# Gate and up passes of a mixture-of-experts layer in four 32-slot column tiles, and a gather that rotates over four PSUM banks

## What is computed

```python
def expert_block(args):
    rows, e = args
    xb = x_pad[rows]
    h = jax.nn.silu(xb @ w_gate[e]) * (xb @ w_up[e])
    return h @ w_down[e]
...
routed = jax.ops.segment_sum(yb * row_g[:, None].astype(yb.dtype), row_t, num_segments=n + 1)[:n]
shared = (jax.nn.silu(xt @ ws_gate) * (xt @ ws_up)) @ ws_down
```

## Time and profile before

| what | value |
|---|---|
| median of 3 runs | 1186.67 us (1184.7 to 1186.79) |
| span of the profiled execution, first to last instruction | 1183.3 us |
| what lies around the span, if that execution took the median | 3.4 us |
| PE matmuls busy | 1149.2 us (97%) |
| weight loads of PE | 688.0 us (58%) |
| VectorE, ScalarE | 347.2 us, 300.0 us |
| DMA | 449.12 MB, mean 380 GB/s |
| MoE of layer 0, gate pass of unit 0 to last down pass | 134 to 572 us |
| MoE of layer 1 | 732 to 1169 us |

### The profile page before, as it was taken

How to read it: one execution, slowest core, us unless ns; L and a number is a source line. 1 busy time by engine, 2 the same in 40 slices (tenths; PEclk the granted TensorE clock), 3 DMA queues, 4 the chain that set the end, 5 groups by cost and what they waited for, 6 DMA issues and landing times.

```text
span 1183.3 us, 22174 instructions
## 1 busy us (share of the span) xinstructions
PE 1149.2 (97%) x8846; PEld 688.0 (58%) x8846; DVE 347.2 (29%) x912; ACT 300.0 (25%) x713; POOL 56.4 (5%) x100
## 2 busy tenths in 40 slices
PE   9999999999999999999999999999999899999995
PEld 6865755555555555554787647555555555555552
DVE  0445522222122212121523557221222222121224
ACT  1454222212122212121214533122221212221222
POOL 1431100000001000000011001000000010000000
PEclk9999999999999999999999999999999999999998
DMA  9945999999999999999990558999999999999995
GB/s 375 418 161 185 349 418 426 428 428 428 429 428 421 429 426 427 426 426 418 406 364 2 230 233 343 408 426 426 429 429 428 428 423 427 426 426 428 428 423 204
DMA packets 42732, 449.12 MB, mean 380 GB/s; under 512 B 4512, under 2 KB 4896, under 8 KB 14240
## 3 DMA queue, kind: packets, MB, share of 16 engines
q1 hardware_dynamic: 41648, 443.30, 89.8%
q10 hardware_dynamic: 1008, 4.73, 1.0%
HBM read 446.96 MB, written 1.05 MB: 379 GB/s over the span
## 4 chain that ended last, share of the span: by engine, by line
PE 85%; DMA 9%; DVE 3%; ACT 1%; issue 1%; DVEq 0%; SPq 0%; ACTq 0%
PE bank L1301 18%; PE bank L1328 17%; PE bank L1364 17%; PE bank L848 7%; PE bank L867 6%; PE bank L1372 5%; PE bank L906 4%; DMA store<-in_w_gate 4%; DMA store<-in_w_down 3%; DMA store<-in_w_in_b 2%; PE bank L1337 2%; PE bank L1196 1%; PE bank L1066 1%; PE bank L1077 1%; ACT work L1498 1%
## 5 line engine op out<-in xcount | busy, mean ns | idle before, releaser
L1301 PE MATMUL bank<-store,work 128*64 128x256 f32 x1984 | 227.8, 382 | 5.3 <-DMA store<-in_w_gate 5.3
L1328 PE MATMUL bank<-store,work 128*64 128x256 f32 x1952 | 225.3, 379 | 6.2 <-issue 6.2
L1364 PE MATMUL bank<-store,work 128*32 128x512 f32 x1888 | 218.4, 595 | 3.1 <-ACT work L1498 2.9
L1301 PEld LDWEIGHTS bank<-store,work 128*64 128x64 f32 x1984 | 137.0, 137 | 116.1 <-issue 41.1
L1328 PEld LDWEIGHTS bank<-store,work 128*64 128x64 f32 x1952 | 145.0, 137 | 75.7 <-issue 11.6
L2030 DVE SCALAR_TENSOR_TENSOR yhalf<-bank,gcol,yhalf 128x512 fp32r<-128x512 f32 x124 | 92.9, 751 | 219.1 <-ACT yhalf L1664 219.1
L2022 DVE TENSOR_TENSOR work<-work,bank 128x256 f32<-128x256 f32 x64 | 27.0, 422 | 346.9 <-PE bank L1328 346.9
L1664 ACT ACTIVATE yhalf<-bank,gcol 128x512 fp32r<-128x512 f32 x124 | 85.1, 688 | 172.1 <-PE bank L1364 172.1
L1364 PEld LDWEIGHTS bank<-store,work 128*32 128x32 f32 x1888 | 56.1, 109 | 122.4 <-issue 110.7
L1498 ACT ACTIVATE work<-bank 128x512 f32<-128x512 f32 (+4 forms) x177 | 78.0, 441 | 105.8 <-PE bank L848 47.3
L1498 ACT ACTIVATE back<-bank 128x128 fp32r<-128x128 bf16 x64 | 17.8, 278 | 282.0 <-PE bank L1269 282.0
(11 more groups left out here) (185 smaller groups left out, 822.7 us busy)
## 6 DMA issues: line engine op xcount, KB each, us to landing
store<-in_w_down SPq DMA_DIRECT2D x56, 2048.0 KB, 17.7
store<-in_w_gate SPq DMA_DIRECT2D x56, 2048.0 KB, 17.7
store<-in_w_up SPq DMA_DIRECT2D x52, 2048.0 KB, 19.2
store<-in_w_up SPq DMA_DIRECT2D x18, 1024.0 KB, 10.5
store<-in_w_gate SPq DMA_DIRECT2D x12, 1024.0 KB, 8.5
store<-in_w_in_b SPq DMA_DIRECT2D x3, 3072.0 KB, 22.4
store<-in_w_out SPq DMA_DIRECT2D x4, 2048.0 KB, 14.2
store<-in_w_down SPq DMA_DIRECT2D x6, 1024.0 KB, 11.7
```

The costliest lines, as they stand in the source:

```text
L1301: last = pe.matmul(gate_bank[slots_of(e), 0:HID], xg[:, k, slots_of(2 * j + e)], w[e][:, k, :], start=(k == 0), stop=(k == KT - 1))
L1328: last = pe.matmul(up_bank[slots_of(e), 0:HID], xg[:, k, slots_of(2 * j + e)], w[e][:, k, :], start=(k == 0), stop=(k == KT - 1))
L1364: last = pe.matmul(yb[half][rows_of(t, e), :], hT[b][:, f, slots_of(e, t)], w[e][:, f, half * 512:half * 512 + 512], start=(f == 0), stop= ...
```

## The change

Gate and up no longer use one 64-column tile for each expert, but two 32-column tiles for each, one for each token tile. The 64 partitions of an expert and their order stay the same, and each 32-slot tile streams the same 256 weight columns. So a pass has 32 products in the code where it had 16.

The gather's chunks take the banks 0, 3, 1, 2, 0, 3, 1, 2 in place of 0, 1, 2, 0, 1, 2, 0, 1. Four waits follow the banks: the wait for `back_ready` and `gcol_ready` (bank 1) moves from chunk 1 to chunk 2, that for `hT_ready` (bank 2) from chunk 2 to chunk 3; the gate pass of an octet's first unit now also waits before its first matmul until chunk 5 (bank 3, which is the gate bank) is copied out; and the two halves of the down pass wait for chunks 4 and 6, both copied out by ScalarE, in place of chunk 6 and VectorE's chunk 7.

```diff
-        gather_bank = (0, 1, 2, 0, 1, 2, 0, 1)
+        gather_bank = (0, 3, 1, 2, 0, 3, 1, 2)
...
                         if k == 2 and backs is not None:
-                            pe.wait_ge(s_("hT_ready"), backs)
-                        if k == 1 and backs is not None:
                             pe.wait_ge(s_("back_ready"), backs + 1)
                             pe.wait_ge(s_("gcol_ready"), backs + 1)
+                        if k == 3 and backs is not None:
+                            pe.wait_ge(s_("hT_ready"), backs)
...
-                def slots_of(e, t=None):
-
-
-                    first, n = (e * SLOTS, SLOTS) if t is None else (e * SLOTS + t * TILE_SLOTS, TILE_SLOTS)
-                    return slice(first, first + n)
+                def slots_of(e, t):
+
+                    first = e * SLOTS + t * TILE_SLOTS
+                    return slice(first, first + TILE_SLOTS)
...
-                        if j == 0 and k == 0 and first:
-                            chunk_out(O, 3)
+                        if j == 0 and k == 0:
+                            chunk_out(O, 3 if first else 5)
...
                         for e in range(2):
-                            last = pe.matmul(gate_bank[slots_of(e), 0:HID], xg[:, k, slots_of(2 * j + e)], w[e][:, k, :],
-                                             start=(k == 0), stop=(k == KT - 1))
+                            for t in range(TT):
+                                last = pe.matmul(gate_bank[slots_of(e, t), 0:HID], xg[:, k, slots_of(2 * j + e, t)], w[e][:, k, :],
+                                                 start=(k == 0), stop=(k == KT - 1))
...
                         for e in range(2):
-                            last = pe.matmul(up_bank[slots_of(e), 0:HID], xg[:, k, slots_of(2 * j + e)], w[e][:, k, :],
-                                             start=(k == 0), stop=(k == KT - 1))
+                            for t in range(TT):
+                                last = pe.matmul(up_bank[slots_of(e, t), 0:HID], xg[:, k, slots_of(2 * j + e, t)], w[e][:, k, :],
+                                                 start=(k == 0), stop=(k == KT - 1))
...
                     for half in range(2):
-                        if half == 0:
-                            pe.wait_ge(s_("xg_act"), 4 * gathers + 1)
-                        else:
-                            pe.wait_ge(s_("xg_dve"), 4 * gathers + 1)
+                        pe.wait_ge(s_("xg_act"), 4 * gathers + half)
+                        if half == 1:
                             pe.wait_ge(s_("back_ready"), turned + 1)
                             pe.wait_ge(s_("gcol_ready"), turned + 1)
```

## The result

The changed kernel takes 1190.5 us (median of 5 runs, 1189.9 to 1191.8), the kernel before beside it 1186.0 us (5 runs): a ratio of 1.0044, 95% interval 1.0032 to 1.0055. It is slower by 5.2 us by that ratio; the forecast was 1188.8 us. The profiled execution has a span of 1190.0 us and took 1191.84 us, so 1.84 us lie around a span, where the forecast had put 3.4.

The account below looks back on a forecast made before the run. The prediction took the full DMA as the bound: +2.4 us for code, -0.17 and -0.1 made +2.1 on a 1183.3 us span, 1185.4, plus 3.4 around it: 1188.8 us. Its 8-in-10 range was 1185.6 to 1192.4 us.

Parts of the forecast that it names:

- The bound: Both MoE layers: the DMA is full at about 427 GB/s; a unit takes 14.7 us to load, 12.23 us on PE.
- the waits marked "issue": PE waits before an up pass, counted as waits for weights within 11.5 us over both layers.
- The rival that PE sets the end: Whole kernel: PE's savings count in full, 14.4 us less, giving 1172.3 us; chance 0.08.
- Part 1: Gate and up passes: 64 matmuls of 128x32 replace 32 of 128x64 at the same stream time, 0 us.
- The rival of 61 ns for one: Gate and up passes: PE can't keep pace for 128 matmuls, 0.45 us more a pass, 1207 us; chance 0.06.
- Parts 2 and 3: Down-to-gate saves 0.17 us at each place, only the last counting (-0.17 us); gather's up to 0.3 us is hidden, 0.
- Part 4: PE's code: 6144 more instructions, about 24 packets of 16 KB; 22 under full DMA cost +2.4 us (0.9 to 3.3).
- my upper bound of 0.15: Code fetch under full DMA: the most one packet costs, in us, around an estimate of 0.11.
- dips in the middle of the MoE: Sign that the forecast is wrong: the DMA rate dips there or falls below 420 GB/s, a lost lead.
- about 13 us of other loads are always queued ahead: DMA queue: a 2 MB load lands 17.7 us after issue but takes 4.9 us, so the DMA has no gaps.
- The wrong 3.4 us: Time around the profiled span, added to 1185.4 us to give 1188.8 us.
- the refetched loop: PE loop over octets 1 to 3: each further pass brings 6 packets again, +2.6 us, 1191.5 us; chance 0.17.

## Why the prediction was right, and what it mis-sized

**The bound: right.** PE has slack against the DMA while the kept pair is 16. PE's gains turned into waits in the changed kernel (28.1 us for 11.5) and with the banks alone (17.8). That the waits marked "issue" are waits for weights, as the forecast assumed, the trace of the changed kernel bears out: the five between 237 and 350 us end at 264.42, 279.11, 308.47, 323.15 and 337.84 us, each 0.09 us after the last part of a 2 MB load has landed, and no code comes in that stretch for which PE could have waited. The rival that PE sets the end fell; it isn't a property of the passes, though, but of this place of the kept pair, as the runs with pair 20 show.

**Part 1, the shape at 0: right.** 64 narrow matmuls are repeated every 3.45 us over two passes. The rival of 61 ns for one would have given 3.9 us, and the estimate that I drew from the Trainium skill, "TensorE: Matmul & The Clock Gate" (Wait — 56ns, not 53.3ns?), 4.0 us. Measured is 3.45 us/64 = 54 ns. So the rival's 61 ns fell, and the 62 ns, which the Trainium skill states there for hardware decode switched off, don't set the pace here; no run shows which setting holds. The forecast's own row gives 16 x 0.22 = 3.5 us for a pass, not quite the 3.45 that it wrote down; the chain's 3.45 us was the better ground.

**Parts 2 and 3: right.** Down to gate is 3.46 us, the unit 12.08 us for 12.05 foreseen, the gather's wait is gone, and the banks cost nothing (0.9996).

**Part 4, the count: right.** 81 packets, 1.33 MB; the loop isn't brought again (6 packets, then none), so that rival fell, and with it, for six blocks too, the rule on a window of two blocks in the Trainium skill, "Runtime: NRT & Kernel Launch" (Instruction fetch mechanics).

**Part 4, the price: the term that was mis-sized.** "22 x 0.11 = +2.4 us (0.9 to 3.3)" should have been about +5. The 0.11 came from the mean rates of two stretches in which the queue was mostly full, and as a mean rate it holds: 0.09 us with the old loop written out. Over the whole kernel a packet costs 5.2/24 = 0.22 us in the changed kernel, 0.22 with its loop written out, 0.29 with the old loop written out. The lower ends of the three intervals (3.8/24, 8.7/47 and 2.8/15: 0.16, 0.18 and 0.19) lie above my upper bound of 0.15. A mean rate counts what all the DMA engines lose together, and PE waits for the part of a load that lands last. The forecast had no term for that, and its dips, at the kept pair and at the end of a layer, it named only as a sign against itself ("dips in the middle of the MoE"). It also held that "about 13 us of other loads are always queued ahead"; where SP issues nothing for 11.7 us (348.83 to 360.58 us in the kernel before) few can be left.

**Around the span: wrong by 1.6 us.** Setting the span of one execution against the median of other runs gave 3.4 us; it is 1.84. The span forecast was 1185.4 us, the one measured 1190.0. With 1.84 us the sum would have read 1187.2: 3.3 us short, of which 2.8 are the price of the packets (5.2 - 2.4). The wrong 3.4 us brought the forecast nearer to the result than its steps deserve, and the upper end of its range, 1192.4 us, was that of the refetched loop, which didn't happen. That the number came out so near is in part luck.

**Left open.** The 2.0 us of the kernel with four tiles only in the loop are more than 4 packets at 0.3 us would make, and no stretch of its profile that was read holds them. A small cost of the shape itself isn't ruled out by that run; with 0.19 to 0.40 us for a packet from the old loop written out, the 24 packets make 4.6 us or more of the change's 5.2 us.

## What to carry to other kernels

Where the DMA queue is full, an edit that writes more instructions is an edit of the DMA: count the instructions in the program's text, not those executed, and price a packet by a run in which only the code grows (a loop written out), since a mean rate of a full stretch shows half of it here. Where a wait needs all parts of a load, look at when the last part lands, not only at GB/s. Filling a dip in the rate gains nothing if the dip is where an older delay comes due: look whether a new one opens at the next place where the queue is low. Before an engine's speed-up is called hidden, look at how near it is to setting the end; here the same passes, with their code, cost 5.2 us with the kept pair at 16 and gained 2.3 us with it at 20.

## What the hardware showed that I had not expected

- Code that is executed once costs 0.2 to 0.3 us for each 16 KB packet beside full weight loads, five or more times what its bytes alone make at the full rate (0.04 us).
- The record of a 16 KB packet of code lasts 1.05 us, 1.7 times that of a 16 KB packet of weights (0.62 us).
- The 16 parts of a load stay apart by the same time for 20 loads and more while the queue is full (2.8 us in the kernel before, 5.7 us in the changed one), drift further apart where code comes, and close up where the queue runs low.
- A copy of one 8 KB row between two places in DRAM was cut into 512-byte pieces, just as one written as 16 rows.
